# Attention value sums with two corner products of 256 columns, and the gate of two steps back moved ahead of a step's maxima

## The reference, cut to what matters

```python
def band_blocks(t):
    tb = t.reshape(B, S // WINDOW, WINDOW, K, Dh)
    prev = jnp.concatenate([jnp.zeros_like(tb[:, :1]), tb[:, :-1]], axis=1)
    return jnp.concatenate([prev, tb], axis=2)          # 256 keys of a block of 128 queries

diff = WINDOW + qi - s                                  # qi: query, s: key, in a block
valid = (diff >= 0) & (diff < WINDOW)                   # exactly 128 keys of the 256 count
...
probs = jax.nn.softmax(jnp.concatenate([logits, sink], axis=-1), axis=-1)[..., :-1]
o = jnp.einsum("bnkgqs,bnskd->bnqkgd", probs, v_band)
return (o * jax.nn.silu(z)) @ w_out
```

## Time and profile before

| what | value |
|---|---|
| time, median of 3 runs | 2231.12 us (2231.07 to 2231.17) |
| span of the profiled execution | 2230.9 us (the page gives no other time of it) |
| PE busy | 2163.5 us, 97% of the span |
| DVE, ACT, POOL busy | 64%, 46%, 46% of the span |
| DMA | 592.86 MB, mean 266 GB/s |

### The profile page before, as it was taken

One profiled execution on the slowest core, in us unless ns is written; L12 is line 12 of the kernel. 1 busy time (PEld: TensorE's weight loads), 2 busy tenths in 40 slices (PEclk: granted clock), 3 DMA queues, 4 the chain that ended last, 5 costly groups with the idle time before them and its releaser, 6 DMA issues.

```text
span 2230.9 us, 28791 instructions
## 1 busy us (share of the span) xinstructions
PE 2163.5 (97%) x10410; PEld 1808.6 (81%) x10410; DVE 1436.8 (64%) x1815; ACT 1032.7 (46%) x1898; POOL 1037.3 (46%) x636
## 2 busy tenths in 40 slices
PE   5999999999999999999999999999999999999998
PEld 4887778788888878888787888887888888888887
DVE  6966548757476864554974653867676657657764
ACT  4334445634545644445644445434444434434442
POOL 2556775845553865544684555440222232232222
PEclk9999999999999999999999999999999999999999
DMA  9888899785559795557876565989677797787554
GB/s 344 307 300 309 310 319 343 236 309 174 201 189 334 277 322 173 197 192 279 312 277 247 179 211 206 353 341 361 226 282 243 260 342 251 268 313 274 196 203 170
DMA packets 244782, 592.86 MB, mean 266 GB/s; under 512 B 20928, under 2 KB 96800, under 8 KB 244256
## 3 DMA queue, kind: packets, MB, share of 16 engines
q1 hardware_dynamic: 241680, 585.71, 72.8%
q10 hardware_dynamic: 2960, 5.30, 0.7%
HBM read 461.96 MB, written 119.54 MB: 261 GB/s over the span
## 4 chain that ended last, share of the span: by engine, by line
PE 74%; DMA 7%; POOL 6%; DVE 5%; ACT 3%; DVEq 2%; POOLq 1%; issue 1%; SPq 1%; ACTq 0%
PE ps L2272 22%; PE ps L2274 22%; PE ps L2273 22%; POOL w_lo L1110 3%; DMA w_raw<-in_a_w_in 2%; PE ps L2477 2%; POOL cbl L1129 1%; PE ps L2527 1%; PE ps L2526 1%; PE ps L2552 1%; DMA zo<-tt 1%; DVE yb L2018 1%; DMA w_raw<-a_weights_combined 1%; DMA r<-b_input 1%; ACT w_hi L1304 1%
## 5 line engine op out<-in xcount | busy, mean ns | idle before, releaser
L1110 POOL TENSOR_TENSOR w_lo<-w_raw,w_hi 128x1024 fp32r<-128x1024 f32 x244 | 650.4, 2684 | 568.8 <-ACT w_hi L1304 568.8
L1304 ACT ACTIVATE w_hi<-w_raw 128x1024 fp32r<-128x1024 f32 x260 | 271.7, 1057 | 413.8 <-DMA w_raw<-in_a_w_in 370.2
L2272 PE MATMUL ps<-h,w_hi 128*128 128x512 f32 x1024 | 403.2, 394 | 10.2 <-POOL w_lo L1110 9.4
L2274 PE MATMUL ps<-h,w_lo 128*128 128x512 f32 x1024 | 398.9, 390 | 0.0
L2273 PE MATMUL ps<-h,w_hi 128*128 128x512 f32 x1024 | 398.7, 389 | 0.0
L1249 POOL TENSOR_SCALAR_AFFINE_SELECT pt<-pt 128x512 fp32r<-128x512 f32 x128 | 82.2, 642 | 395.4 <-ACT pt L1666 338.9
L2272 PEld LDWEIGHTS ps<-h,w_hi 128*128 128x128 f32 x1024 | 192.2, 188 | 55.5 <-POOL w_lo L1110 14.7
L2274 PEld LDWEIGHTS ps<-h,w_lo 128*128 128x128 f32 x1024 | 192.2, 188 | 40.6
L2273 PEld LDWEIGHTS ps<-h,w_hi 128*128 128x128 f32 x1024 | 192.4, 188 | 38.9 <-issue 0.2
L2272 PE MATMUL ps<-r,w_hi 128*128 128x512 f32 x480 | 191.7, 399 | 3.8 <-ACT kvf L1608 2.3
L2274 PE MATMUL ps<-r,w_lo 128*128 128x512 f32 x480 | 187.7, 391 | 0.0
(11 more groups left out here) (268 smaller groups left out, 4636.8 us busy)
## 6 DMA issues: line engine op xcount, KB each, us to landing
w_raw<-in_a_w_in SPq DMA_DIRECT2D x256, 256.0 KB, 3.6
w_hi<-b_weights_split SPq DMA_DIRECT2D x104, 512.0 KB, 4.4
w_lo<-b_weights_split SPq DMA_DIRECT2D x104, 512.0 KB, 5.8
w_raw<-in_a_w_in SPq DMA_DIRECT2D x52, 512.0 KB, 4.9
w_raw<-in_a_w_out SPq DMA_DIRECT2D x48, 512.0 KB, 5.7
w_hi<-v_weights_combined SPq DMA_DIRECT2D x48, 512.0 KB, 4.0
w_lo<-v_weights_combined SPq DMA_DIRECT2D x48, 512.0 KB, 5.1
w_hi<-a_weights_combined SPq DMA_DIRECT2D x32, 512.0 KB, 6.3
```

Source lines behind the costliest of these rows:

```text
L1110: g.tensor_tensor(wlo[p][:, rows_], raw[p][:, rows_], whi[p][:, rows_].bitcast(F32), ALU.subtract).then_inc(w_lo, 1)
L1304: s_.activation(whi[p][:, rows_], raw[p][:, rows_], ACT.Copy).then_inc(w_hi, 1)
L2272: t_.matmul(dst_, stat[0], mov[0], start=start, stop=False)
L2274: return t_.matmul(dst_, stat[1], mov[0], start=False, stop=stop)
```

## The change

The value sum is written with another split of the square. The base of a query is no longer v_before for all keys: for the keys 0 to 63 it is v_here, for the keys 64 to 127 it is v_before. What is then wrong are two triangles: among the first 64 queries the keys above q (tile `edge_low`), among the last 64 queries those up to q (`edge_up`), together with the other half in each, so that each corner product has 128 partitions and 4 heads of 64 queries, 256 columns. In each corner product the 128 partitions hold 64 keys twice, with p hi in one half and p lo in the other, so hi and lo need one matmul in place of two. The tiles `pt` 2 and 3 and `dst` are gone; `p_edge`, `edge_low` and `edge_up` are new. VectorE writes the lo halves of `p_edge` itself, GpSimd masks four pieces of 64x256 in place of two of 128x512 and takes over the lo part of the two edge tiles (`edge_rest`), and ScalarE's `kv_round` has 7 instructions in place of 3. Several tiles move to other addresses, and `keep` and its making are gone. On VectorE `gated_output(n-2)` stands at the start of slot n.

```diff
             def mask(a):
-                for m, ready in ((0, pt_hi), (1, pt_lo)):
-                    pool.wait_ge(ready, a + 1)
-                    last = g.affine_select(out=pt[:, 2 + m]..., in_=pt[:, m]..., ...)
-                last.then_inc(pt_masked, 1)
+                high = pt[:, 0].rearrange("p (h q) -> p h q", h=4)
+                pool.drain()
+                pool.wait_ge(pt_hi, a + 1)
+                kept(p_edge[64:P, 1], high[64:P, :, HEAD:P], True)
+                kept(p_edge[0:64, 0], high[0:64, :, 0:HEAD], False)
+                pool.wait_ge(pt_lo, a + 1)
+                kept(p_edge[0:64, 1], p_edge[0:64, 1].rearrange("p (h q) -> p h q", h=4), True)
+                kept(p_edge[64:P, 0], p_edge[64:P, 0].rearrange("p (h q) -> p h q", h=4), False).then_inc(pt_masked, 1)
+                pool.wait_ge(pt_masked, a + 1)
+            def edge_rest(g_, kh):
+                pool.drain()
+                pool.wait_ge(kv_hi_done, at("kv_hi_done", g_, kh + 1))
+                for n, (edge, here) in enumerate(((edge_up, slice(64, P)), (edge_low, slice(0, 64)))):
+                    for there in (slice(0, 64), slice(64, P)):
+                        last = g.tensor_tensor(edge[there, :, kh, HEAD:P], df[here],
+                                               edge[here, :, kh, 0:HEAD].bitcast(F32), ALU.subtract)
+                    if n == 0:
+                        pool.drain()
+                last.then_inc(edge_lo, 1)
+                pool.drain()
...
                 s_.activation(ks[rows_, kh, 0, P:5 * P], kw[rows_, :], ACT.Copy)
-                s_.activation(vst[:, 1:5, kh, 0:HEAD], kvf[:, 1:5, cols_], ACT.Copy)
-                s_.activation(dst[:, :, kh, 0:HEAD], df[:], ACT.Copy).then_inc(kv_hi_done, 1)
+                s_.activation(vst[0:64, :, kh, 0:HEAD], kvf[0:64, 1:5, cols_], ACT.Copy)
+                s_.activation(vst[64:P, :, kh, 0:HEAD], kvf[64:P, 0:4, cols_], ACT.Copy)
+                for there in (slice(0, 64), slice(64, P)):
+                    s_.activation(edge_low[there, :, kh, 0:HEAD], df[0:64], ACT.Copy)
+                    last = s_.activation(edge_up[there, :, kh, 0:HEAD], df[64:P], ACT.Copy)
+                last.then_inc(kv_hi_done, 1)
...
             for s, slot in enumerate(SLOTS):
                 a = s - PRO_SLOTS
+                if 0 <= a - 2 < ATT:
+                    gated_output(a - 2)
                 if 0 <= a < ATT:
...
-                    v.tensor_tensor(pt[:, 1, :], bank(6), pt[:, 0, :].bitcast(F32), ALU.subtract).then_inc(pt_lo, 1)
-                if 0 <= a - 2 < ATT:
-                    gated_output(a - 2)
+                    v.tensor_tensor(pt[:, 1, :], bank(6), pt[:, 0, :].bitcast(F32), ALU.subtract).then_inc(pt_all, 1)
+                    v.tensor_tensor(p_edge[64:P, 0]..., turned_p[0:64, :, 0:HEAD], high[0:64, :, 0:HEAD], ALU.subtract)
+                    v.tensor_tensor(p_edge[0:64, 1]..., turned_p[64:P, :, HEAD:P],
+                                    high[64:P, :, HEAD:P], ALU.subtract).then_inc(pt_lo, 1)
...
-                pe.wait_ge(pt_masked, a + 1)
                 if a >= 1:
                     pe.wait_ge(o_done, a)
+                pe.wait_ge(pt_hi, a + 1)
                 t_.matmul(bank(7), vst[:, blk, kh, :], pt[:, 0, :], start=True, stop=False)
+                pe.wait_ge(pt_all, a + 1)
                 t_.matmul(bank(7), vst[:, blk, kh, :], pt[:, 1, :], start=False, stop=False)
-                t_.matmul(bank(7), dst[:, blk, kh, :], pt[:, 2, :], start=False, stop=False)
-                t_.matmul(bank(7), dst[:, blk, kh, :], pt[:, 3, :], start=False, stop=True).then_inc(pv_full, 1)
+                pe.wait_ge(edge_lo, at("edge_lo", g, kh + 1))
+                pe.wait_ge(pt_masked, a + 1)
+                by_query = bank(7).rearrange("p (h q) -> p h q", h=4)
+                t_.matmul(by_query[:, :, 0:HEAD], edge_low[:, blk, kh, :], p_edge[:, 0, :], start=False, stop=False)
+                t_.matmul(by_query[:, :, HEAD:P], edge_up[:, blk, kh, :], p_edge[:, 1, :], start=False, stop=True) \
+                    .then_inc(pv_full, 1)
```

More of the change, by code:

```diff
@@ L442, in yoco_kernel @@
         zg = place("zg", v_at, [KT, T], F32)
[L443 to L445 removed]
+        pt = place("pt", v_at + 16 * K, [2, 512], F32R)
+        p_edge = place("p_edge", v_at + 22 * K + 64, [2, 4 * HEAD], F32R)
+        edge_low = place("edge_low", v_at + 24 * K + 64, [NC, KVH, P], F32R)
+        pp = [place(f"pp{n}", at_, [4, P + 1], F32) for n, at_ in enumerate((v_at + 28 * K + 64, v_at + 20 * K))]
+        obt = place("obt", v_at + 30 * K + 128, [2, P], F32)
         xs = place("xs", x_at, [NC, D], F32)
@@ L477, in yoco_kernel @@
         gate_b = place("gate_b", gb_at, [D], F32)
-        wh = [place(f"wh{n}", w_at, [T], F32) for n, w_at in enumerate((wh_at, wh_at + 2 * K, v_at + 29 * K + 512))]
+        wh = [place(f"wh{n}", w_at, [T], F32) for n, w_at in enumerate((wh_at, wh_at + 2 * K, gt + 14 * K))]
         tt = [place(f"tt{n}", ga_at + 2 * K * n, [T], F32) for n in range(2)]
@@ L513, in yoco_kernel @@
         ident = place("ident", region(512), [P], F32)
-        ones = place("ones", region(512), [P], F32)
-        keep = place("keep", region(512), [P], F32)
+        ones_at = region(1024)
+        ones = place("ones", ones_at, [P], F32)
+        ot = place("ot", ones_at, [2, P], F32)
         prev = place("prev", region(512), [P], F32)
@@ L1253, in mask, with kept @@
-                last.then_inc(pt_masked, 1)
+                def kept(there, in_, low):
+                    heads = there.rearrange("p (h q) -> p h q", h=4)
+                    if low:
+                        return g.affine_select(out=heads, in_=in_, compare_op=ALU.is_ge, fill=0.0, base=0,
+                                               pattern=[[0, 4], [1, HEAD]], channel_multiplier=-1)
+                    return g.affine_select(out=heads, in_=in_, compare_op=ALU.is_gt, fill=0.0, base=0,
+                                           pattern=[[0, 4], [-1, HEAD]], channel_multiplier=1)
@@ L1283, in _ @@
                     normalise(a)
-                for pc in slot:
+                    if a % STEPS == 3:
+                        edge_rest(a // STEPS, 1)
+                for k, pc in enumerate(slot):
                     tasks(pc)
+                if s and keys_in(s - 1) is not None:
+                    edge_rest(keys_in(s - 1), 0)
             for pc in range(B_PIECES, B_PIECES + 6):
```

39 lines of the change are left out of this document (19 added, 20 removed).

## The result

The changed kernel takes 2253.36 us, the median of four runs (2251.14 to 2253.71), against 2231.14 for the kernel before on the same chip. The ratio is 1.0102, with a 95% interval of 1.0088 to 1.0116. It is 1% slower; 2231.5 was forecast, with a range up to 2242. The profiled execution took 2253.2, with a span of 2251.5 us, 20.6 longer than before.

A forecast was written before the change was run, and what follows sets the result against it. TensorE was taken as the bound, busy 2163.5 of 2230.9 us. 2230.9 - 13.9 (matmul gain) + 14.3 (new waits) = 2231.3, median 2231.5 us; range 2221 to 2242, own range 2227 to 2235 (chance 0.40).

The forecast's parts named there:

- The gain of the matmuls: Layer B's value sums: two matmuls of 512 columns become two of 256, 0.217 us a step, 13.9 over 64 steps.
- The corner waits: TensorE waits for GpSimd's masks at the corners, mainly in late slots; 14.3 us taken, between 9 and 17.
- carrying: Late maxima delay exponentials, reciprocal, rotary sums and the next gate, raising waits from about 9 to about 17 us.
- signs of being wrong: Wrong if TensorE's waits for masks at the corners are under 9 or over 18 us, or corners start 0.2 us apart.
- The key and value slots: Longer ScalarE rounding and GpSimd subtractions: TensorE waits 2.3 us in slot 29; VectorE 1.4 longer in 3, 19, 35, 51.
- The clock: Behind a wait of about 3 us some matmuls run at 1.2, not 2.4 GHz, costing some 1.4 us more each.
- The slower rival: Late gates carry on and VectorE and GpSimd block each other: 24 us of waits, 2241.2 us, chance 0.26.
- The meetings of VectorE and GpSimd: VectorE's sums and GpSimd's second masks block each other, 0.9 us each, 7 us more in about eight late slots.

The follow-up runs named there:

- e8: e7 with ScalarE's four edge copies moved to a later point and GpSimd's four edge subtractions run a slot or two later; 2219.89 us, ratio 0.9964.
- e7: e1 without VectorE's two subtractions of 64x256, GpSimd's masks cutting the lo part out of the whole p lo tile; 2230.67 us, ratio 1.0008.
- e1: The changed kernel with the gate put back behind the p lo subtractions, the two corners kept; 2242.89 us, ratio 1.0057.
- e4: The kernel before with its third and fourth value matmul cut to 256 columns, half of the correction left out; 2219.77 us, ratio 0.9954.
- e2: The kernel before with only the gate moved ahead of the maxima; 2242.41 us, ratio 1.0059.
- e9: e8 with the gate moved ahead of the maxima again and nothing else changed; 2229.43 us, ratio 0.9994.

## Why the prediction was wrong

Read backwards from e8, the experiments lead in single steps to the changed kernel, each as a difference of two excesses:

| step | excess | cost |
|---|---|---|
| corners, nothing late (e8) | -8.7 | -8.7 |
| key and value preparation early and long (e7) | 2.1 | +10.8 |
| two subtractions on VectorE (e1) | 13.3 | +11.2 |
| gate ahead of the maxima (changed kernel) | 22.2 | +8.9 |

The rows are measured kernels; that the costs add up is so by construction. In the other order they differ: done alone on the kernel before, the three cost 11.5, 23.4 and 12.9, 47.8 together and not 30.9; slots such as 27 and 44 are late in several of them. The forecast for the three together was 14.3.

**The gain of the matmuls.** The price per matmul was right: starts 0.12 us apart. The step from "13.9 us of matmuls" to "13.9 us of span" was too simple. e4 gave 9.8 and e8 8.7: TensorE arrives earlier and meets transfers that had been in time, above all the one of slot 8 in e4, 3.8 us with its clock. The forecast let the new waits be eaten by old ones, not the gain by new ones.

**The corner waits.** 14.3 us were forecast, with over 18 named as what would refute it; 16.6 were measured, in 15 waits of at most 1.8 us. In slot 54 it was 1.28, where 0.8 and 0.9 more by carrying were forecast. This step held, if not slot by slot: the slots 30 and 36 had none, and the longest was 1.8 and not 2 to 3. None of the signs of being wrong that the prediction named came up; it was wrong at a place that it didn't watch.

**Where else TensorE waits: the step that failed.** The sum put every new wait at the corners. It followed late maxima through p lo and the masks to the value sums, and through the rotary sums to the next gate, but not to ScalarE's copies out of PSUM, which stand behind the exponentials and ahead of TensorE's projections. In numbers: `kvf` 2.3 to 7.9 us, `zg` 1.0 to 4.7, p lo itself 0 to 2.6. Together 11.9 us, less 3.6 for the gate wait that went away, against nothing in the forecast. Of the 11.9 the exponentials' queue has 7.0 (`kvf` 5.6, `zg` of slot 7 1.4), the key roundings of slot 35 have 2.4 and p lo 2.6.

e2 and e9 show this queue with the gate alone. But the gate isn't all of it: `kvf` is 2.7 us in e7, 5.7 in e1 and 7.9 in the changed kernel, so VectorE's two subtractions give it 3.0 and the gate 2.2. The forecast took the subtractions, with their handover, only as 1.0 us more ahead of the masks, and what carries over from the gate's 1.3 us alone. That the 0.84 us of VectorE's time in every step also delay all that stands behind them was put at nothing; they cost 11.2 us by e1 and e7.

**The key and value slots.** The prediction said that in slots 3, 19, 35 and 51 VectorE waits 1.4 us longer and that this "is no wait of TensorE by itself". In slot 35 VectorE waits 2.0 us longer (3.04 for 1.03), and it is one, of 2.37 us. Two sizes were off as well, shown by these groups of layer B (count, busy us, mean ns, idle before):

```profile
L1250 POOL TENSOR_SCALAR_AFFINE_SELECT p_edge<-p_edge 64x256 fp32r<-64x256 f32 x64 | 32.3, 504 | 3.1
...
L2270 DVE TENSOR_TENSOR p_edge<-ps,pt 64x256 fp32r<-64x256 f32 x64 | 26.7, 417 | 2.0
...
L1269 POOL TENSOR_TENSOR edge_up<-df,edge_up 64x256 fp32r<-64x256 f32 x16 | 14.5, 905 | 48.5 <-ACT edge_up L1676 48.0
...
L1269 POOL TENSOR_TENSOR edge_low<-df,edge_low 64x256 fp32r<-64x256 f32 x16 | 11.8, 740 | 1.6
L1675 ACT ACTIVATE edge_low<-df 64x256 fp32r<-64x256 f32 x16 | 6.7, 417 | 0.2
```

A rounding of 64x256 takes 0.42 us and the next starts 0.43 later, where 0.3 to 0.4 was taken. GpSimd's subtraction takes 0.74 to 0.91, where 0.6 was taken between bounds of 0.41 and 1.04. In slot 29 the first rounding starts at 1840.22 and the last subtraction ends at 1846.56, 6.3 us where the forecast has 1839.2 - 1834.17 = 5.0. The corners waited 1.17 us there all the same, at the lower end of the 1.2 to 4. In e7 it is 2.38 us, and 2.0 more at the value sums just before. The whole of the key and value work cost 10.8 us (e8 to e7), not the 2.3 of slot 29 and what it carries.

**The clock.** 1.4 us more were named for each wait of 3 us, and none stands in the sum. It was 5.3 us in all, 26 more matmuls of 512 columns at the lower of TensorE's two levels (1.2 GHz): behind the waits of 3.97 and 3.93 us in the slots 27 and 44, and behind the one of 2.37 in slot 35, but not behind the one of 2.35 in slot 7.

**The slower rival.** It gave 2241.2, from 24 us of additional waits. These were 34.7 - 11.0 = 23.7, so its sum of waits was right, but partly by luck, as 11.9 us of them stand at places that it doesn't name. The other 12 us are:

- 5.3: the clock.
- 2.6: the 0.16 us by which a wait costs more than its row says, for 25 waits in place of 9.
- 1.1: layer B's first slot starts later. That moves from kernel to kernel, between 3.1 us earlier (e4) and 1.9 later (e9), though layer A's work is the same.
- 1.5: the execution that was profiled before. In every run on record that has both, the time is 1.7 to 1.8 us above the span. So that execution took about 2232.6 us, 1.5 above the median, and the 0.2 us between the span and the median before compare two different executions.
- About 2 us that stay open.

The meetings of VectorE and GpSimd it spoke of are there, in L2166 of slot 35 and in the 504 ns mean of L1250, but no run took them away alone, so their share of the time isn't known.

Of the three theories behind the experiments each holds in part: in the order of the table the gate's place, the key and value preparation and the added VectorE time are each about a third of the 31 us, and none is enough alone.

## What to carry to other kernels

When an instruction is put ahead of others on an in-order engine, follow the delay through every queue that waits for any of them, here ScalarE's exponentials and what stands behind them, not only to the consumer that the change has in mind. Work added to a nearly full in-order engine delays all that stands behind it, not only its own result: two subtractions of 0.42 us a step cost 11 us here, though with them (e1) TensorE waited only 1.7 us at the corners that need their result. Count a saving on the bounding engine as less than its matmul time where transfers are only just in time and the DMA engines are full. Helper work that isn't due yet belongs behind the urgent work, as in e8, where the same copies on ScalarE and subtractions on GpSimd a slot or two later were worth 10.8 us, and a copy that another engine's masking can do on its way is best not made at all.

## What the runs showed of the hardware

- GpSimd's selection reads one half of the partitions and writes the other at the price of one that stays: 0.41 us for 64x256. The following one, of slot 24 of e8, crosses over:

```profile
1776.36 0.41 POOL L1247 TENSOR_SCALAR_AFFINE_SELECT p_edge<-pt 64x256 fp32r<-64x256 f32 x1 [0.46 <-DVE pt L2271]
```

- ScalarE's copies of 64x256 in `kv_round` take 0.42 us each and start 0.41 to 0.43 us apart; one of 128x256 has a row of 0.40, and behind L1647 the next starts 0.30 to 0.32 later. So splitting a copy by partitions more than doubles its time.
- VectorE's subtraction of 64x256 that reads two SBUF tiles takes 0.42 us when GpSimd is idle, 0.86 to 0.87 beside GpSimd's edge subtractions, 0.53 beside its selections and 1.17, once, beside the multiplication L1279. This is the second of its kind in `kv_rest`, in the changed kernel, where `edge_rest` runs beside five of the eight, and in e8, where it comes later and GpSimd is idle beside all eight (count, ns least, median, most; first and last start):

```profile
L2168 DVE TENSOR_TENSOR vst<-kvf,vst x8: 532/868/1173, 1521.0 to 2097.0; 64x256 fp32r<-64x256 f32 x8
```

```profile
L2174 DVE TENSOR_TENSOR vst<-kvf,vst x8: 422/422/423, 1517.8 to 2069.8; 64x256 fp32r<-64x256 f32 x8
```

  A subtraction that reads PSUM and one SBUF tile wasn't slowed, as the prediction had it. L2270's mean of 417 ns says little, as only 7 of the 128 of L2270 and L2272 ran beside GpSimd (417 to 427 ns). The p lo subtraction says more: 30 of its 64 ran beside GpSimd in the changed kernel and 47 in e8, and all of them took 678 to 693 ns.
